# Unused bytes between SBUF buffers: activations and attention outputs at other distances from the weights, modulo 256

## The reference, cut to what matters

```
x = x + 0.5 * swiglu(rms_norm(x), w_gate, w_up, w_down)          # D_FF = 2816
h = rms_norm(x); proj = h @ w_in                                  # q, k, v, c_q, c_kv, k_rope, two gates
o_a = sliding-window attention, 8 heads of 64, with ALiBi and sinks
o_b = multi-head latent attention, 8 heads, low-rank q and kv, rotary part
x = x + (sigmoid(g_a) * (o_a @ w_branch_a) + sigmoid(g_b) * (o_b @ w_branch_b)) @ w_out
x = x + 0.5 * swiglu(rms_norm(x), ...)                            # second FFN
```

## Time and profile before

| | |
|---|---|
| median of 3 runs | 1044.41 us (1044.19 to 1044.72) |
| the profiled execution | 1044.15 us, span 1042.4 us |
| busy: PE, PEld, DVE, ACT, POOL | 1037.6, 897.7, 718.0, 585.8, 62.8 us |
| granted TensorE clock, mean | 1.000 |
| DMA | 187.60 MB, mean 180 GB/s |

### The profile page before, as it was taken

How to read it: one execution, slowest core, us unless ns; L and a number is a source line. 1 busy time by engine, 2 the same in 40 slices (tenths; PEclk the granted TensorE clock), 3 DMA queues, 4 the chain that set the end, 5 groups by cost and what they waited for, 6 DMA issues and landing times.

```text
span 1042.4 us, 15577 instructions
## 1 busy us (share of the span) xinstructions
PE 1037.6 (100%) x5656; PEld 897.7 (86%) x5656; DVE 718.0 (69%) x1132; ACT 585.8 (56%) x935; POOL 62.8 (6%) x69
## 2 busy tenths in 40 slices
PE   9999999999999999999999999999999999999998
PEld 8888888998888888888888888889988888888887
DVE  6766666668786876666686666666688868676665
ACT  6555455466963754554565455455678646454552
POOL 1052000112100000000000000001211000000000
PEclk9999999999999999999999999999999999999999
DMA  7765544455435455555545555634454346545541
GB/s 265 247 222 188 207 163 166 138 182 190 150 122 202 168 189 192 206 186 204 180 147 202 201 187 182 213 130 151 160 202 162 122 162 222 202 162 200 191 172 61
DMA packets 35269, 187.60 MB, mean 180 GB/s; under 512 B 4496, under 2 KB 4640, under 8 KB 20128
## 3 DMA queue, kind: packets, MB, share of 16 engines
q1 hardware_dynamic: 34704, 186.03, 51.0%
q0 software_dynamic: 240, 0.53, 0.2%
q10 hardware_dynamic: 288, 0.54, 0.2%
HBM read 186.04 MB, written 1.05 MB: 179 GB/s over the span
## 4 chain that ended last, share of the span: by engine, by line
PE 99%; DVE 0%; issue 0%; ACT 0%; DVEq 0%; ACTq 0%
PE ps L1364 96%; PE ps L1784 1%; PE ps L1388 1%; PE ps L1375 1%; PE ps L1811 1%; PE ps L1847 0%; PE ps L1694 0%; DVE hT L1000 0%; PE ps L1686 0%; PE ps L1412 0%; DVE x L993 0%; ACT hT L602 0%; DVE w_lo L911 0%; PE ps L1400 0%; DVE kTA L863 0%
## 5 line engine op out<-in xcount | busy, mean ns | idle before, releaser
L1364 PE MATMUL ps<-hT,w_hi 128*128 128x512 f32 x1408 | 341.5, 391 | 0.2 <-DVE hT L1000 0.2
L1364 PEld LDWEIGHTS ps<-hT,w_hi 128*128 128x128 f32 x1408 | 259.0, 188 | 50.3 <-DVE hT L1000 0.5
L878 DVE TENSOR_TENSOR w_lo<-w_raw,w_hi 128x2048 fp32r<-128x2048 f32 x82 | 188.0, 2293 | 87.3 <-ACT w_hi L541 87.3
L1364 PEld LDWEIGHTS ps<-hT,w_lo 128*128 128x128 f32 x1408 | 180.9, 191 | 7.4
L1364 PE MATMUL ps<-hT,w_lo 128*128 128x256 f32 x1408 | 182.9, 283 | 0.0
L1364 PE MATMUL ps<-w_hi,hT 128*128 128x512 f32 (+2 forms) x576 | 174.6, 377 | 0.0
L541 ACT ACTIVATE w_hi<-w_raw 128x2048 fp32r<-128x2048 f32 x85 | 161.9, 1905 | 13.4 <-PE ps L1364 13.2
L1364 PE MATMUL ps<-w_lo,aTh 128*128 128x512 f32 x352 | 137.1, 389 | 0.0
L1364 PE MATMUL ps<-w_hi,aTl 128*128 128x512 f32 x352 | 137.0, 389 | 0.0
L1364 PE MATMUL ps<-w_hi,aTh 128*128 128x512 f32 x352 | 136.8, 390 | 0.0
L570 ACT ACTIVATE S<-ps 128x256 f32<-128x256 f32 x88 | 33.7, 383 | 159.3 <-PE ps L1364 159.3
(11 more groups left out here) (166 smaller groups left out, 958.8 us busy)
## 6 DMA issues: line engine op xcount, KB each, us to landing
w_raw<-in_w_ffn SPq DMA_DIRECT2D x85, 1024.0 KB, 4.9
w_raw<-in_w_ffn SPq DMA_DIRECT2D x92, 512.0 KB, 5.6
w_raw<-in_w_gate SPq DMA_DIRECT2D x16, 1024.0 KB, 4.9
w_raw<-in_w_proj SPq DMA_DIRECT2D x16, 592.0 KB, 4.8
w_raw<-in_w_branch SPq DMA_DIRECT2D x8, 1024.0 KB, 4.7
w_raw<-in_w_out SPq DMA_DIRECT2D x8, 1024.0 KB, 4.8
w_raw<-in_w_uq SPq DMA_DIRECT2D x4, 384.0 KB, 2.9
SG<-in_w_ffn SPq DMA_DIRECT2D x1, 1024.0 KB, 10.6
```

What stands on the lines that cost most here:

```text
L878: dve.tensor_tensor(wl_gu[b], raw_gu[b], wh_gu[b].bitcast(F32), ALU.subtract).then_inc(lo_gu.sem, 1)
L1364: return pe.matmul(dst, w, m, start=start, stop=stop, skip_group_check=True)
```

## The change

Seven unused tensors (`pad_h`, `pad_a` to `pad_f`, of 16, 56, 16, 40, 48, 20 and 60 float32 a partition, that is 64, 224, 64, 160, 192, 80 and 240 bytes) are declared between the others. Nothing reads or writes them. hT then starts 64 bytes past a multiple of 256 from the start of `w_raw`, aTh 32, aTl 96, oTh 192 and oTl 16. The first four pads have 512 bytes together and the last three 512 too, so all other tensors keep their distance modulo 256; work to S lie 512 bytes further on, SG and what follows 1024.

```diff
         x = sb("x", [P, TT, D_MODEL])
+        pads = [sb("pad_h", [P, 16])]
         hT = sb("hT", [P, KC, 2, SEQ], F32R)
         hTh, hTl = hT[:, :, 0, :], hT[:, :, 1, :]
+        pads.append(sb("pad_a", [P, 56]))
         aTh = sb("aTh", [P, 2, SEQ], F32R)
+        pads.append(sb("pad_b", [P, 16]))
         aTl = sb("aTl", [P, 2, SEQ], F32R)
+        pads.append(sb("pad_c", [P, 40]))
         work = sb("work", [P, 4 * SEQ])
...
         S = sb("S", [P, HB, SEGS * P])
         folded = S[:, :, :].rearrange("p h n -> p (h n)")[:, 4 * HALF:6 * HALF].rearrange("p (b s n) -> p b s n", b=2, s=2)
+        pads.append(sb("pad_d", [P, 48]))
         oTh = sb("oTh", [P, 8, SEQ], F32R)
+        pads.append(sb("pad_e", [P, 20]))
         oTl = sb("oTl", [P, 8, SEQ], F32R)
+        pads.append(sb("pad_f", [P, 60]))
         SG = sb("SG", [P, KC, HALF])
```

## The result

The changed kernel takes 1051.2 us (median of 6 runs, 1050.99 to 1051.54); the kernel before took 1044.14 us beside it (6 runs). The ratio is 1.0067 with a 95% interval from 1.0056 to 1.0078. The forecast was 1044.4 us, no change, with 0.14 for slower. The time lies inside the stated range and near the 1050.4 us of rival 2, but the likeliest case was wrong.

What follows compares the result with a forecast made beforehand. PE, busy for 100% of the span, bounds the kernel through its matmul pitches. The profiled execution's 1044.15 us plus terms of 0, with the median 0.26 us above it, gave 1044.4 us; range 1041 to 1052.

Steps and rivals of the forecast that it cites:

- rival 2: Gate and up, rest by their weights: new distances put streams out of step, 1.2 ns each, 1050.4 us for all; chance 0.14.
- the likeliest case: Whole kernel: no change in time, 1044.4 us, own range 1043.5 to 1045.5; chance 0.69.
- What bounds the kernel, and that only the pitch can move: PE is busy for 100% of 1042.4 us, so the change acts only through the time between matmul starts.
- The constant of 13.3 ns as the only place where a conflict could hide: Each split-operand matmul's pitch beyond its columns, 13.3 ns; 66.5 us over 5000 matmuls.
- Price of another distance: 0, so 5000 x 0 = 0 us: All 5000 split-operand matmuls: a changed distance between operands costs 0 ns each, 0 us in all.
- The row: Attention products of branches A and B, weights at distance 128 and 0: both runs of 32 last 2.82 us, so price 0.
- The upper end, 1.2 ns on 5000, from the 416-column rows: 416-column split products run unevenly, 1.2 ns above the constant; on 5000 matmuls that is 6 us more.
- 3680 matmuls at distance 64, one price for all: Of 5000 split-operand matmuls, 3680 were counted at distance 64, all priced at 0 ns like the others.
- The excess behind a low run, left as it is since nothing in it names an address: 512-column matmuls right behind a low run: some 0.02 us a block over 88 blocks, 2 us in all, taken as unchanged.
- Rival 1: Split products: moving reads and weight loads collide, distance frees them; 978 us fully, 1027 for aT or oT weights only; chance 0.17.
- Rival 3: Tensor places might be rounded up to 64 bytes, so three of five distances differ; 1044.4 us, within no change's 0.69.
- The two pages: Skill pages on PE: one gives about 2.5 ns beside the columns, the other two independent read ports, keeping the sum at 0.

Runs made afterwards that it cites:

- aT_32_96_alone: Only aTh (32 bytes) and aTl (96) moved off the multiples of 256, against the kernel before, hT and oT staying at 0: 1051.3 us, ratio 1.0064.

## Why the prediction was wrong, step by step

- *What bounds the kernel, and that only the pitch can move*: right. DVE and ACT stayed at 718.1 and 585.9 us, and the added time is all PE's own.
- *The constant of 13.3 ns as the only place where a conflict could hide*: right in that the pitch is what moved, wrong in that it is one constant. What remains beside the columns went from 6.6 ns (113.3 - 106.7) to 20.7 (234 - 213.3), and at one distance the two lengths can move in opposite ways: at +32 a 512-column step takes 6 ns more and a 256-column one 2 less.
- *Price of another distance: 0, so 5000 x 0 = 0 us*. This is the step that failed. Measured, the changed kernel's distances cost 5.4 us in `down`, 2.6 in the mixer and 2.1 in the high steps, and gave back 3.3 in the low ones; with 0.5 us in the rest that is the 7.3 us of the span. The row was read rightly: branch A's and B's products are still equal in the changed kernel, and ident, now 32 bytes off, still transposes S in 1.47 us for twelve, as at distance 0:

```profile
272.12 1.47 PE L1784 MATMUL ps<-ident,S 128*128 128x128 f32 x12
```

```profile
274.01 1.47 PE L1791 MATMUL ps<-ident,S 128*128 128x128 f32 x12
```

  But those are plain float32, and the split products are another kind of matmul (no run tells whether it is the type or the shape that makes the difference). The prediction named this limit and chose the row all the same. No row of the kernel before had a split product at another distance, so none could tell: between ends 72 us apart the trace allowed a range of both signs, and no price.
- *The upper end, 1.2 ns on 5000, from the 416-column rows*: the total was near (7.1 us, 1.4 ns), the place was not. Rival 2 put the cost in gate and up and less in down; measured, gate and up together lose nothing (+2.1 high, -3.3 low), and down has 5.4 us of the 7. By size it was a mean over terms of both signs, so the agreement is luck. The 416-column steps from which the price came did not follow the distance either: by w_hi they went from 188.2 ns to 187.0.
- *3680 matmuls at distance 64, one price for all*: the 864 with hT as weights are at -64, and the sign counts. They rose to 233 ns, the high ones to 229.5, and the low ones fell.
- *The excess behind a low run, left as it is since nothing in it names an address*: such excess depends on addresses too. In aT_32_96_alone it makes 1.8 us in high steps that are themselves at distance 0.
- *Rival 1*: its direction is real as well. Low steps at +64 lose up to 6 of 13 ns, and with aT on the grid the kernel is faster than before. The part that it priced by itself, 17.6 us for aT and oT as weights, did not come: `down` has its lowest mean, 227.1 ns, with aT on the grid.
- *Rival 3*: half true. Places are rounded up, to 32 bytes; it moved oTl to 32 in place of 16, and SG and ident to 32; nothing in the 7 us is seen to come from it.
- *The two pages*: the Trainium skill, "SBUF — State Buffer" (Who interferes with whom), gives PE two independent read ports. The runs do not bear out that this means no price: shifting both operands changes nothing, shifting one costs up to 18 us. Where a page and a measurement differ, the measurement decides. By "TensorE: Matmul & The Clock Gate" of the Trainium skill (Wait — 56ns, not 53.3ns?), the constant is 2.5 ns; no distance that was run brings a float32r step there, the least being 6.6 ns.

What stays open is the mechanism: which two reads meet, why 256-column steps are cheapest at 64 and 192 and 512-column ones at 0, and why the end of the high run chooses the pitch of the low one. The runs show the rule, not the circuit.

## What to carry to other kernels

Where PE is the bound and float32r matmuls reload their weights each time, the places of the two operands modulo 256 are a parameter worth a sweep: from 1039 to 1062 us here, with no instruction added or moved. Sweep each pair of tensors alone and then together, because the pitch of a series hangs also on the series before it, and give one tensor two views where its two uses want different places. A row that excludes an effect counts only for the kind of matmul that it shows.

## What the runs showed of the hardware

- Pitch of back-to-back float32r matmuls with new weights each: 226.7 ns for 512 columns and 119.9 for 256 at distance 0 (granted clock 1.00), up to 234 and down to 113.3 at others. The period is 256 bytes and the sign counts.
- Low steps at distance 64 have two steady pitches, 113.3 and 117.8 ns, over 32 matmuls on end, at the same addresses. Where high and low steps are both at +64, all 175 unbroken low runs follow the last pitch of the high run ahead: 113.3 ns behind 231 or 232, 117.8 behind 225 or 226.
- Plain float32 transposes show none of it: twelve take 1.47 us at distance 0 and at 32. The attention products of branch A and B, at 128 and 0, last 2.82 us both.
